# Matrix memory scores from stacked key parts over 128 rows, and the triangle added to the stabilisers once per head

## What is computed

```
def step(carry, inp):
    c_st, n_st, m_st = carry
    q_, k_, v_, i_, f_ = inp
    b = jnp.cumsum(f_, axis=-1)
    d_intra = jnp.where(causal, b[..., :, None] - b[..., None, :] + i_[..., None, :], -jnp.inf)
    m_inter = b + m_st[..., None]
    m_t = jnp.maximum(m_inter, jnp.max(d_intra, axis=-1))
    s = jnp.einsum('bhtd,bhsd->bhts', q_, k_) * jnp.exp(d_intra - m_t[..., None])
    inter = jnp.exp(m_inter - m_t)
    num = jnp.einsum('bhts,bhse->bhte', s, v_) + inter[..., None] * jnp.einsum('bhtd,bhde->bhte', q_, c_st)
    den = jnp.sum(s, axis=-1) + inter * jnp.einsum('bhtd,bhd->bht', q_, n_st)
    h_out = num / jnp.maximum(jnp.abs(den), jnp.exp(-m_t))[..., None]
```

## Time and profile before

| | |
|---|---|
| median of 3 runs | 1285.48 us (1284.33 to 1286.17) |
| the profiled execution's own time | 1285.19 us |
| its span | 1283.4 us |
| TensorE matmuls busy | 1269.3 us, 99% of the span |
| VectorE busy | 698.9 us, 54% |
| ScalarE busy | 404.8 us, 32% |
| GpSimd busy | 745.6 us, 58% |
| DMA | 117.88 MB, 92 GB/s mean |
| chain that ended last | 93% TensorE, 5% VectorE |

### The profile page before, as it was taken

The page is one execution under the profiler, slowest core; times in us unless marked ns, Lnnn a source line. Parts: engine busy times, 40 slices in busy tenths (PEclk is TensorE's granted clock), DMA queues, the critical chain, the costliest instruction groups (busy, mean ns, idle before and its releaser), DMA issues.

```text
span 1283.4 us, 16634 instructions
## 1 busy us (share of the span) xinstructions
PE 1269.3 (99%) x6664; PEld 1044.4 (81%) x6664; DVE 698.9 (54%) x952; ACT 404.8 (32%) x738; POOL 745.6 (58%) x441
## 2 busy tenths in 40 slices
PE   8999999999999999999999999999999999999998
PEld 6888877888888888888888778778988888888886
DVE  5453564867544432113466879685777764447003
ACT  4333474322111111002346355483532221110002
POOL 6854533576666656768665545223369666666660
PEclk9999999999999999999999999999999999999999
DMA  7222211333333323323333222102133233322331
GB/s 289 82 66 83 82 51 50 101 97 99 99 99 98 99 67 111 100 91 127 99 101 96 67 73 76 51 17 69 63 132 99 99 99 99 99 94 91 97 98 66
DMA packets 34241, 117.88 MB, mean 92 GB/s; under 512 B 3812, under 2 KB 4388, under 8 KB 34036
## 3 DMA queue, kind: packets, MB, share of 16 engines
q1 hardware_dynamic: 32832, 114.51, 27.5%
q10 hardware_dynamic: 1332, 2.31, 0.5%
HBM read 114.71 MB, written 2.10 MB: 91 GB/s over the span
## 4 chain that ended last, share of the span: by engine, by line
PE 93%; DVE 5%; issue 1%; DMA 0%; ACT 0%; POOL 0%; DVEq 0%; SPq 0%; ACTq 0%
PE PS L489 28%; PE PS L491 28%; PE PS L490 28%; PE PS L1104 1%; PE PS L709 1%; PE PS L989 1%; PE PS L686 1%; DVE AL L1852 1%; PE PS L697 1%; PE PS L521 1%; PE PS L522 1%; PE PS L526 1%; DVE ACC L1862 1%; PE PS L576 1%; DVE TMP L2292 1%
## 5 line engine op out<-in xcount | busy, mean ns | idle before, releaser
L439 POOL TENSOR_TENSOR WL<-RAW,WH 128x1024 fp32r<-128x1024 f32 (+1 forms) x207 | 487.7, 2356 | 17.3
L436 POOL TENSOR_SCALAR WH<-RAW 128x1024 fp32r<-128x1024 f32 (+1 forms) x207 | 222.4, 1075 | 413.1 <-DMA RAW<-in_w 371.2
L489 PE MATMUL PS<-AH,WH 128*128 128x512 f32 x896 | 351.6, 392 | 1.9 <-DVE AL L1852 1.9
L491 PE MATMUL PS<-AH,WL 128*128 128x512 f32 x896 | 348.8, 389 | 0.0
L490 PE MATMUL PS<-AL,WH 128*128 128x512 f32 x896 | 348.7, 389 | 0.0
L489 PEld LDWEIGHTS PS<-AH,WH 128*128 128x128 f32 x896 | 168.2, 188 | 40.7 <-DVE AL L1852 2.7
L491 PEld LDWEIGHTS PS<-AH,WL 128*128 128x128 f32 x896 | 168.2, 188 | 35.2
L490 PEld LDWEIGHTS PS<-AL,WH 128*128 128x128 f32 x896 | 168.3, 188 | 34.6 <-issue 0.5
L1434 ACT ACTIVATE TMP<-PAD,PRM 128x512 f32<-128x512 f32 x44 | 35.9, 816 | 120.5 <-DVE PAD L2107 120.5
L489 PE MATMUL PS<-WH,SH 128*128 128x512 f32 x176 | 68.5, 389 | 0.0
L489 PE MATMUL PS<-SH,WH 128*128 128x512 f32 x176 | 68.5, 389 | 0.0
(11 more groups left out here) (376 smaller groups left out, 2099.0 us busy)
## 6 DMA issues: line engine op xcount, KB each, us to landing
RAW<-in_w SPq DMA_DIRECT2D x185, 512.0 KB, 3.6
RAW<-in_w SPq DMA_DIRECT2D x16, 384.0 KB, 3.1
RAW<-in_w SPq DMA_DIRECT2D x16, 320.0 KB, 2.8
X<-in_x SPq DMA_DIRECT2D x4, 512.0 KB, 6.6
BT<-in_bias SPq DMA_DIRECT2D x1, 2048.0 KB, 8.2
out<-FX SPq DMA_DIRECT2D x4, 256.0 KB, 2.1
out<-FX ACTq DMA_DIRECT2D x4, 256.0 KB, 2.0
PIN<-in_p ACTq DMA_DIRECT2D x1, 512.0 KB, 3.3
```

Source lines behind the costliest of these rows:

```text
L436: nc.gpsimd.tensor_scalar(WH[:, slot, 0:width], RAW[:, slot, 0:width], 1.0, 1.0, ALU.mult, ALU.mult).then_inc(s_hi, 1)
L439: nc.gpsimd.tensor_tensor(WL[:, slot, 0:width], RAW[:, slot, 0:width], WH[:, slot, 0:width].bitcast(F32), ALU.subtract).then_inc(s_split, 1)
L489: nc.tensor.matmul(o, lh, rh, start=start, stop=False)
L491: return nc.tensor.matmul(o, ll, rh, start=False, stop=stop)
```

## The change

- Scores: for each head the 64 rows of rounded keys and the 64 rows of their low parts are stacked on 128 partitions (`KS`). The queries' high part stands twice, on both halves (`QD`), their low part once, over zeros (`QZ`). A score tile is then two matmuls that contract over 128 rows, in place of three over 64; the sum of products is the same.
- Making these operands: for the first pair of heads ScalarE writes six 64-row tiles (two of keys, four of queries) in place of two 128-row ones, and VectorE makes four 64-row subtractions and two memsets in place of two 128-row subtractions, before the loop. For the second pair GpSimd makes all of it, twelve instructions behind its last weight unit of the stage, in place of ScalarE (`score_high(1)`) and VectorE (`score_low(1)` at n = 3).
- Exponents: `exponents(n)` is gone. Once per head VectorE adds the triangle to the head's stabilisers from PSUM for all four tiles and both directions (`stabilisers_masked`, one instruction of 128x1024, into `MASKED`), and ScalarE adds the key constant as the bias of its diagonal exponential. The masked instruction of head h + 1 stands at n = 2, 6, 10, ahead of `weighted(n - 1)`, and waits for ScalarE's copies of the same stabilisers.
- `state_sum(2)` moves from behind the loop to n = 15, ahead of `weighted(15)`. GpSimd's `YL` no longer waits for the exponents.

```diff
-        KQH = (put("KQH0", [P, 2, T], F32R, R + 24 * KB), put("KQH1", [P, 2, T], F32R, A_at + 8 * KB))
-        AKL = put("AKL", [P, 2, T], F32R, R + 52 * KB)
-        AQL = put("AQL", [P, 2, T], F32R, A_at + 28 * KB)
+        KS = (put("KS0", [P, 2, T], F32R, R + 24 * KB), put("KS1", [P, 2, T], F32R, A_at + 8 * KB))
+        QD = ((put("QD0", [P, T], F32R, R + 50 * KB), put("QD1", [P, T], F32R, PAD_at)),
+              (put("QD2", [P, T], F32R, A_at + 12 * KB), put("QD3", [P, T], F32R, A_at + 14 * KB)))
+        QZ = ((put("QZ0", [P, T], F32R, R + 52 * KB), put("QZ1", [P, T], F32R, A_at + 28 * KB)),
+              (put("QZ2", [P, T], F32R, A_at + 22 * KB), put("QZ3", [P, T], F32R, A_at + 24 * KB)))
+        UPPER, LOWER = slice(0, HD), slice(HD, P)
+        MASKED = (put("MASKED0", [P, 2, T], F32, R), put("MASKED1", [P, 2, T], F32, R + 4 * KB))
...
-            split_range(UNITS["ffn"][0] + 3, UNITS["wo2"][0] + 4)
+            split_range(UNITS["ffn"][0] + 3, UNITS["wo2"][0] + 3)
+
+            split_range(UNITS["wo2"][0] + 3, UNITS["wo2"][0] + 4)
+            pool.wait_ge(s_aqk, 4)
+            pool.wait_ge(s_gs, 2 * NT)
+            pool.wait_ge(s_split, UNITS["wo2"][0] + 4)
+            for e, (own, far) in enumerate(((UPPER, LOWER), (LOWER, UPPER))):
+                done = 6 * e
+                if e:
+                    pool.wait_ge(s_pk, done)
+                nc.gpsimd.tensor_scalar(KS[1][own, e, :], AK[own, 1, :], 1.0, 1.0, ALU.mult, ALU.mult).then_inc(s_pk, 1)
+                pool.wait_ge(s_pk, done + 1)
+                nc.gpsimd.tensor_tensor(KS[1][far, e, :], AK[own, 1, :], KS[1][own, e, :].bitcast(F32), ALU.subtract
+                                        ).then_inc(s_pk, 1)
+                pool.wait_ge(s_pk, done + 2)
+                nc.gpsimd.tensor_scalar(QD[1][e][own], AQ[own, 1, :], 1.0, 1.0, ALU.mult, ALU.mult).then_inc(s_pk, 1)
+                pool.wait_ge(s_pk, done + 3)
+                nc.gpsimd.tensor_scalar(QD[1][e][far], AQ[own, 1, :], 1.0, 1.0, ALU.mult, ALU.mult).then_inc(s_pk, 1)
+                pool.wait_ge(s_pk, done + 4)
+                nc.gpsimd.tensor_tensor(QZ[1][e][own], AQ[own, 1, :], QD[1][e][own].bitcast(F32), ALU.subtract
+                                        ).then_inc(s_pk, 1)
+                pool.wait_ge(s_pk, done + 5)
+                nc.gpsimd.memset(QZ[1][e][far].bitcast(F32), 0.0).then_inc(s_pk, 1)
+            pool.wait_ge(s_pk, 12)
             pool.wait_ge(s_bsr, 1)
             for h in range(H2):
                 y = YB[:, h, :].rearrange("p (i c) -> p i c", i=NT)
                 r = BSS[:, NT * h:NT * h + NT].rearrange("p (i o) -> p i o", o=1).to_broadcast([P, NT, DV])
                 nc.gpsimd.tensor_tensor(y, y, r, ALU.mult).then_inc(s_ybr, 1)
-            pool.wait_ge(s_ad, 2 * NT * H2)
...
@@ -1007,6 +1035,7 @@
                     ge(pe, s_msl, 2)
                 else:
                     pe.wait_ge(s_bcc, 2 * h)
+                    pe.wait_ge(s_masked, h)
...
@@ -1073,18 +1102,18 @@
 
             def lstm_scores(n):
                 h, j = divmod(n, NT)
-                hp, ht = (h % 2) * HD, h // 2
+                e, ht = h % 2, h // 2
                 if n == 0:
                     pe.wait_ge(s_sao, 2 * NT)
                 if n >= 2:
                     pe.wait_ge(s_sw, 2 * (n - 1))
-                if n in (0, 2 * NT):
-                    ge(pe, s_kql, 2 * ht + 2)
-                r = slice(hp, hp + HD)
-                kh, qh, kl, ql = KQH[ht][r, 0, :], KQH[ht][r, 1, :], AKL[r, ht, :], AQL[r, ht, :]
-                nc.tensor.matmul(pb[2 + n % 2], kh[:, tokens(j)], qh, start=True, stop=False)
-                nc.tensor.matmul(pb[2 + n % 2], kl[:, tokens(j)], qh, start=False, stop=False)
-                nc.tensor.matmul(pb[2 + n % 2], kh[:, tokens(j)], ql, start=False, stop=True).then_inc(s_ms2, 1)
+                if n == 0:
+                    ge(pe, s_kql, 6)
+                if j == 0 and ht:
+                    pe.wait_ge(s_pk, 6 * (e + 1))
+                keys = KS[ht][:, e, tokens(j)]
+                nc.tensor.matmul(pb[2 + n % 2], keys, QD[ht][e][:], start=True, stop=False)
+                nc.tensor.matmul(pb[2 + n % 2], keys, QZ[ht][e][:], start=False, stop=True).then_inc(s_ms2, 1)
...
-            def score_high(ht):
-                for w, src in enumerate((AK, AQ)):
-                    act.wait_ge(s_aqk, ht + (3 if w == 0 else 1))
-                    A(KQH[ht][:, w, :], src[:, ht, :], ACT.Copy).then_inc(s_kqh.sem, 1)
+            def keys_high():
+                act.wait_ge(s_aqk, 3)
+                for e, own in enumerate((UPPER, LOWER)):
+                    A(KS[0][own, e, :], AK[own, 0, :], ACT.Copy).then_inc(s_kqh.sem, 1)
+
+            def queries_high():
+                act.wait_ge(s_aqk, 1)
+                for e, own in enumerate((UPPER, LOWER)):
+                    for half in (UPPER, LOWER):
+                        A(QD[0][e][half], AQ[own, 0, :], ACT.Copy).then_inc(s_kqh.sem, 1)
...
-            score_high(0)
+            keys_high()
             near_copied(NT)
+            queries_high()
...
-                    act.wait_ge(s_ad, 2 * NT * (h - 1))
                     act.wait_ge(s_w, 2 * NT * (h - 1))
...
-            act.wait_ge(s_gs, 2 * NT)
-            score_high(1)
...
+                    if j == 0:
+                        act.wait_ge(s_masked, h + 1)
                     for d in range(2):
-                        act.wait_ge(s_ad, 2 * n + d + 1)
-                        A(WT[:, n % 3, d, tokens(j)], WT[:, n % 3, d, tokens(j)], ACT.Exp).then_inc(s_w, 1)
+                        c = CG[:, j, d, h + H2 * d:h + H2 * d + 1]
+                        A(WT[:, n % 3, d, tokens(j)], MASKED[h % 2][:, d, tokens(j)], ACT.Exp, bias=c
+                          ).then_inc(s_w, 1)
...
+            def score_low():
+                ge(dve, s_kqh, 6)
+                for e, (own, far) in enumerate(((UPPER, LOWER), (LOWER, UPPER))):
+                    V_.tensor_tensor(KS[0][far, e, :], AK[own, 0, :], KS[0][own, e, :].bitcast(F32), ALU.subtract
                                      ).then_inc(s_kql.sem, 1)
+                for e, own in enumerate((UPPER, LOWER)):
+                    ge(dve, s_kql, e + 1)
+                    V_.tensor_tensor(QZ[0][e][own], AQ[own, 0, :], QD[0][e][own].bitcast(F32), ALU.subtract
+                                     ).then_inc(s_kql.sem, 1)
+                for e, far in enumerate((LOWER, UPPER)):
+                    ge(dve, s_kql, e + 2)
+                    V_.memset(QZ[0][e][far].bitcast(F32), 0.0).then_inc(s_kql.sem, 1)
...
                 if n == NT + 1:
-                    score_low(0)
+                    score_low()
...
+            def stabilisers_masked(h):
+                dve.wait_ge(s_bcc, 2 * h + 2)
+                if h >= 2:
+                    dve.wait_ge(s_w, 2 * NT * (h - 1))
+                V_.tensor_tensor(MASKED[h % 2].rearrange("p d (j c) -> p d j c", j=NT),
+                                 PS[:, 0:2, :].rearrange("p d (j c) -> p d j c", j=NT),
+                                 NEG.rearrange("p d (o c) -> p d o c", o=1).to_broadcast([P, 2, NT, P]), ALU.add
+                                 ).then_inc(s_masked, 1)
+
...
             dve.wait_ge(s_go, 2 * NT)
-
-            def exponents(n):
-
-                h, j = divmod(n, NT)
-                if j == 0:
-                    dve.wait_ge(s_bcc, 2 * h + 2)
-                if n >= 3:
-                    dve.wait_ge(s_mo, n - 2)
-                for d in range(2):
-                    c = CG[:, j, d, h + H2 * d:h + H2 * d + 1]
-                    V_.scalar_tensor_tensor(WT[:, n % 3, d, tokens(j)], STAB[h % 2][:, d, tokens(j)], c, NEG[:, d, :],
-                                            ALU.add, ALU.add).then_inc(s_ad, 1)
+            stabilisers_masked(0)
...
             for n in range(NT * H2 + 1):
                 if n in (3, 10):
                     gate_read(2 if n == 3 else 3)
-                if n < NT * H2:
-                    exponents(n)
+                if n % NT == 2 and n // NT < H2 - 1:
+                    stabilisers_masked(n // NT + 1)
                 if n:
                     weighted(n - 1)
                     if n % NT == 1 and n > NT:
                         state_out(n // NT - 1)
-                    if n in (7, 11):
+                    if n in (7, 11, 15):
                         if n < 2 * NT:
                             dve.wait_ge(s_ms2, 2 * NT)
...
-                if n == 3:
-                    score_low(1)
...
-            state_sum(H2 - 2)
             state_out(H2 - 1)
-            V_.memset(PAD[:, 1, 0:1], 0.0)
+            V_.memset(PAD[:, :, 0:1], 0.0)
```

More of the change, by code:

```diff
@@ L135, in build @@
         TMP = put("TMP", [P, 4, T], F32)
+        PAD_at = base[0]
         PAD = put("PAD", [P, 2, T + 2], F32)
@@ L349, in build @@
         s_ybr = sem("s_ybr")
+        s_pk, s_masked = sem("s_pk"), sem("s_masked")
         s_y2p = sem("s_y2p")
@@ L380, in build @@
```

(5 more changed lines are left out.)

4 lines of the change are left out of this document (removed).

## The result

The change made the kernel slower: 1292.18 us, median of 6 runs (1291.53 to 1292.86), against 1285.05 (1284.33 to 1286.17) for the kernel before, measured beside it. The ratio is 1.0054 with a 95% interval of 1.0044 to 1.0065. The prediction was 1286.1, its range 1282.0 to 1290.0: wrong by 6.1 us, and outside its range. The profiled execution took 1292.86, with a span of 1291.0 (before: 1285.19 and 1283.4), so 7.6 us of span are to be found.

What follows compares the result with a forecast made beforehand. TensorE bounds the kernel, with VectorE and ScalarE nearly full: 9.0 us saved, 9.9 given back in waits, 0.3 regained at `YL`, net +0.6 on 1285.19, plus 0.3 for the median: 1286.1 us, range 1282.0 to 1290.0.

Steps and rivals of the forecast that it cites:

- The saving on TensorE: Score tile and mix pairs: 0.56 less each, 9.0 us in all, 3.7 for the third matmul, 5.3 for changes of rows.
- The rival that the changes of rows cost what they did: Scores and mixes: a pair saves only 0.23, so 1287.9 us; chance 0.08.
- Steps 1 to 3: Before mix(2): ScalarE's exponentials and copies, then VectorE's masked instruction and squares, give back 1.5 us, 0.45 of it for GpSimd's packing.
- Step 6: Before mix(5): ScalarE's chain, then the masked instruction and half of `weighted(5)`, leave TensorE standing for 4.0 us.
- Step 10: Before mix(9): the same chain without the tanh, 6.2 against 4.1 of TensorE work, gives back 2.1 us.
- Steps 13 to 15: From mix(11) to the stage's end: ScalarE's chain, `state_sum(2)` and `weighted(15)` give back 2.0 us, 0.6 for `YL` blocking.
- the rival of twice the price: VectorE's masked instruction takes about twice the price, 3.2 us more: 1289.3, slower; chance 0.10.
- The granted clock of 1.00: TensorE in the stage: the clock stays full behind the waits, so the forecast costs no fall.
- The rival had the mechanism: The clock falls in the wait of step 6, to 1.2 GHz, costing 3.7 us: 1289.8, slower; chance 0.12.
- Costed at nothing: VectorE's and ScalarE's added work before the loop fits idle time, to 0.1; GpSimd's packing, 9 us, is ready; dropped exponents gain nothing.
- `YL` (-0.3): Output projection: TensorE's wait of 0.3 for VectorE's `YL` goes.
- the first rival: TensorE stays the bound: 9.0 and the tail's 0.3 are gained, 1276.8 us; chance 0.12.

Runs made afterwards that it cites:

- the run with all waits filled: Changed kernel plus 32 score matmuls that nothing reads, in TensorE's waits before mix(5), mix(9) and mix(15): 1288.41 us, 3.8 less than the changed kernel.
- experiment 4: Each part alone, against the kernel before: two-matmul scores 1285.73 us (1284.25 with GpSimd's packing held back); masked instruction with the old scores 1294.75 us.

## Why the prediction was wrong

**The saving on TensorE (9.0): right.** In the run with all waits filled, start-to-start distances without waits give 5.2 less for the sixteen score tiles, 2.4 for the mixes, 0.7 for gates and 0.7 for turns beside them: 9.0. The rival that the changes of rows cost what they did is refuted by 1.03 to 1.22 for a mix, where it had 1.31. The rule of the Trainium skill (TensorE: Matmul & The Clock Gate, Part 3), that weight loads overlap only when the row group differs, does not hold in these rows: scores, gates and mixes are all full height, and the distance is the shorter 0.23.

**The waits (9.9 given back): right in place and kind, 1.5 low in sum.** First gate 0.3: 0.4. Steps 1 to 3, 1.5: 1.4 (0.66 and 0.73); the 0.45 set there for GpSimd's packing did not come, for the one square that it slowed (0.87) had 1.42 us of VectorE's idle time behind it. Step 6, 4.0: 4.3, by the very chain that was written out. Step 10, 2.1: 2.4. Steps 13 to 15, 2.0: 2.9 (0.3, 2.2 and 0.4); here `state_sum(2)` took 2.15 beside GpSimd's `YL` where 1.14 and 0.6 had been set. The masked instruction took 1.23, where 1.25 was estimated, so the rival of twice the price falls. The sum is 11.4.

**The granted clock of 1.00: the step that failed.** The wait of 4.0 at step 6 was foretold with its length, and then the matmuls behind it were costed at full clock. The reason given was the one long wait of the trace before, 2.0 us at the very start, behind which the clock column reads 1.00. The rows of that place say something else (timeline; all records of line 644, in ns shortest, median and longest; windows as above):

```profile
1.99 5.81 PE L644 MATMUL PS<-PAD 128*128 128x256 f32 x16 [1.99 <-DVE PAD L1880]
...
L644 PE MATMUL PS<-PAD x16: 379/634/792, 2.0 to 7.4; 128*128 128x256 f32 x16
...
2.00:4.00 2.00, 2.00 (x5) 1.64 (x6) 0.00 (x0) 0.67 (x2) 0.00 (x0) 1.00 0.83 229
6.00:8.00 2.00, 1.80 (x8) 1.27 (x6) 0.75 (x1) 1.62 (x3) 1.92 (x3) 1.00 1.02 418
```

These are 16 equal matmuls. Read one by one, they start 0.43 apart from 2.57 to 5.99 us, and 0.21 to 0.22 from 6.34 on: half speed, then full. This trace's record of the clock begins only at 6.3 us, and the view counts what lies ahead of it as 1.00. So the slow state stood in the trace before, and the column hid it. It does not settle what a wait in the middle of work does, since TensorE had done nothing ahead of this one. But it was no evidence for a full clock behind a wait, and there was no other.

The rival had the mechanism, and a chance of 0.12, and the prediction named a dip of the clock as a sign of being wrong. The rival's price of 3.7 for the fall at step 6 was high for this kernel (2.8, 1.5 and 2.4 in three profiles, since the clock comes back on the way), but it had one fall where each profile has two: the waits of 2.1 and 2.0 at steps 10 and 15 were not asked the same question. By the filled waits the falls are worth 3.8 of the miss of 6.1. The Trainium skill (same page, Part 1) says that throttled is the default and activity releases it; the trace agrees: 0.50 behind 4.3 us of standing, 1.00 when those waits are filled.

**Costed at nothing.** Ahead of the stage about 0.5 was lost, not 0.1: the first scores start at 817.50 against 816.98. The first gate starts at 817.94 to 819.42 in the kernels with the new operands, 818.7 to 819.1 in most, against 818.26 before; with the old operands and the masked part alone it is 818.60. It varies with the execution, and its place was not pinned down. The packing took 11.1 us (822.94 to 834.03), not 9, and was ready; in the changed kernel it did not reach the path, since the exponents that it slows were gone. That was not seen in the prediction, and it is a part of why the two parts do not add up (experiment 4).

**`YL` (-0.3): right.**

**The sum.** 1286.1, plus 1.5 for waits, 3.8 for the clock and 0.5 ahead of the stage, is 1291.9; measured were 1292.2. One slip changes nothing in this: the first rival's 1276.8 takes its 9.3 off the forecast; off the kernel before it is 1276.2.
